# The output shift of a fused decoder layer: from VectorE's loop to rows written early and accumulating stores of GpSimd

## What is computed

```
x = x + gt1 * mix
h2 = modulate(rmsnorm(x, norm2_g), sh2, sc2)
ffn = hierarchical_moe(h2, ...)
x = x + gt2 * ffn
mod_f = silu(c) @ w_ada_final + b_ada_final
sh_f, sc_f = split(mod_f, 2)
out = modulate(rmsnorm(x, norm_f_g), sh_f, sc_f)

def modulate(hf, shift, scale):
    return hf * (1.0 + scale) + shift
```

## Time and profile before

| | before |
|---|---|
| median of three runs | 1040.6 us |
| the profiled execution's own time | 1039.79 us |
| its span, first to last instruction | 1038.0 us |
| busy: TensorE / VectorE / ScalarE / GpSimd | 981.2 / 797.5 / 530.4 / 109.1 us |
| mean granted TensorE clock | 0.992 of full speed |
| bytes moved by DMA | 206.78 MB |
| tail: first `YG` load issued | 992.6 us |
| tail: TensorE's first and last weighted sum | 998.2 and 1027.6 us |
| tail: VectorE's last instruction ends | 1034.85 us |

### The profile page before, as it was taken

How to read it: one execution, slowest core, us unless ns; L and a number is a source line. 1 busy time by engine, 2 the same in 40 slices (tenths; PEclk the granted TensorE clock), 3 DMA queues, 4 the chain that set the end, 5 groups by cost and what they waited for, 6 DMA issues and landing times.

```text
span 1038.0 us, 15568 instructions
## 1 busy us (share of the span) xinstructions
PE 981.2 (95%) x5698; PEld 771.5 (74%) x5698; DVE 797.5 (77%) x1486; ACT 530.4 (51%) x930; POOL 109.1 (11%) x151
## 2 busy tenths in 40 slices
PE   5899998999899999999999999899999999999996
PEld 5669688978897998989988888466666666666642
DVE  7859879836983886958676768898888888787828
ACT  4555532654275555555663323465665656565522
POOL 0201101000100000010010000121221221212100
PEclk9899999999999999999999999999999999999998
DMA  9823633232324233230185434589999999999375
GB/s 364 250 80 105 199 105 103 62 101 61 105 61 122 82 93 111 62 102 1 58 333 164 183 141 182 186 292 363 372 370 367 372 366 358 368 355 349 105 306 205
DMA packets 81033, 206.78 MB, mean 199 GB/s; under 512 B 11878, under 2 KB 40630, under 8 KB 72780
## 3 DMA queue, kind: packets, MB, share of 16 engines
q1 hardware_dynamic: 59232, 156.25, 41.8%
q0 software_dynamic: 15120, 43.72, 13.2%
q10 hardware_dynamic: 6620, 6.00, 1.8%
HBM read 189.61 MB, written 24.71 MB: 206 GB/s over the span
## 4 chain that ended last, share of the span: by engine, by line
PE 66%; DVE 15%; DMA 10%; ACT 4%; issue 3%; SPq 1%; ACTq 0%; DVEq 0%; POOLq 0%
PE PS L1999 13%; PE PS L2001 12%; PE PS L2000 12%; DMA WGU<-in_w_exp_up 7%; PE PS L2297 4%; PE PS L2083 3%; PE PS L2305 3%; PE PS L2303 3%; PE PS L2304 3%; DVE AT L1466 3%; PE PS L2288 2%; PE PS L2408 1%; DVE ACC L1264 1%; DMA AST<-in_w_ada 1%; PE PS L2133 1%
## 5 line engine op out<-in xcount | busy, mean ns | idle before, releaser
L1999 PE MATMUL PS<-WH,HT 128*128 128x256 f32 x512 | 146.8, 287 | 1.3 <-ACT GVH L924 1.3
L2000 PE MATMUL PS<-WL,HT 128*128 128x256 f32 x512 | 144.8, 283 | 0.0
L2001 PE MATMUL PS<-WH,HL 128*128 128x256 f32 x512 | 144.8, 283 | 0.0
L1825 DVE TENSOR_TENSOR WGL<-WGU,WGH 128x1024 fp32r<-128x1024 f32 x96 | 116.9, 1219 | 18.1 <-ACT WGH L1171 16.8
L1466 DVE COPY_PREDICATED AT<-MASK,PS 128x64 f32<-128x64 uint8 x320 | 72.8, 228 | 63.1 <-PE PS L2094 44.0
L1171 ACT ACTIVATE WGH<-WGU 128x1024 fp32r<-128x1024 f32 x96 | 98.5, 1064 | 33.6 <-DMA WGU<-in_w_exp_up 28.1
L1999 PEld LDWEIGHTS PS<-WH,HT 128*128 128x128 f32 x512 | 98.2, 192 | 4.0 <-issue 4.0
L2000 PEld LDWEIGHTS PS<-WL,HT 128*128 128x128 f32 x512 | 98.2, 192 | 0.0
L2001 PEld LDWEIGHTS PS<-WH,HL 128*128 128x128 f32 x512 | 98.1, 192 | 0.0
L2303 PE MATMUL PS<-WGH,XGTH 128*96 128x512 f32 x192 | 88.3, 460 | 0.0
L1863 DVE TENSOR_TENSOR WDL<-WDN,WDH 128x2048 fp32r<-128x2048 f32 x32 | 73.4, 2293 | 17.6 <-ACT WDH L1181 17.5
(11 more groups left out here) (355 smaller groups left out, 2259.0 us busy)
## 6 DMA issues: line engine op xcount, KB each, us to landing
WGU<-in_w_exp_gate SPq DMA_DIRECT2D x32, 1024.0 KB, 12.6
WGU<-in_w_exp_up SPq DMA_DIRECT2D x32, 1024.0 KB, 18.5
WDN<-in_w_exp_down SPq DMA_DIRECT2D x32, 1024.0 KB, 13.5
AR<-in_w_ada POOLq DMA_DIRECT2D x32, 512.0 KB, 4.2
WF<-in_w_in SPq DMA_DIRECT2D x28, 512.0 KB, 5.6
AST<-in_w_ada SPq DMA_DIRECT2D x16, 512.0 KB, 8.6
AR<-in_w_ada_final POOLq DMA_DIRECT2D x16, 512.0 KB, 4.7
YG<-expert_rows SPq DMA_DIRECT2D x8, 1024.0 KB, 12.3
```

What stands on the lines that cost most here:

```text
L1825: V.tensor_tensor(WGL[s][:, :, ks, :], WGU[s][:, :, ks, :], WGH[(NCH * s + c) % 4][:].bitcast(F32), ALU.subtract).then_inc(wgl_ready, 1)
L1999: MM(ps, wh, xh, start=first, stop=False)
L2000: MM(ps, wh, xl, start=False, stop=False)
L2001: return MM(ps, wl, xh, start=False, stop=last)
```

## The change

The final shift is no longer added by VectorE. Instead:

- GpSimd's queue, behind its last `store_gain`, waits until all six gains are stored and then issues eight DMAs, DRAM to DRAM, each writing row 2 of `gain_d` (the shift) into the 128 output rows of one tile (4 KB a row, 512 KB a DMA).
- At the end of its program, behind `extras_done`, GpSimd waits for those eight (`shift_st`), and then for each tile waits for `out_scaled` and issues the store of `OUTT[t % 4]` with `accum_op=add`: the DMA adds what it brings to what stands in the output.
- SP's eight plain stores, VectorE's `shifted`, the semaphore `out_ready`, the tile `SHF` and its load on ScalarE's queue are gone. VectorE's wait for `rows_in` is 16 in place of 32.

```diff
@@ sync
             for t in range(NT):
                 sp.dma_start(YG[t][:, :, :], ys_rows[:, 0:3:2, t, :]).then_inc(yg_in[t], 16)
-            for t in range(NT):
-                sp.wait_ge(out_ready, t + 1)
-                sp.dma_start(out_rows[:, t, :], OUTT[:, t % 4, :]).then_inc(out_st[t % 4], 16)
             for s in range(4):
                 sp.wait_ge(out_st[s], 16 * NT // 4)
@@ gpsimd
             for i, g in ((1, GT2), (2, SHC), (3, GSC)):
                 store_gain(i + 2, i, g)
+            pool.wait_ge(gain_st, 96)
+            for t in range(NT):
+                pool.dma_start(out_rows[:, t, :], gain_d[2:3, :].to_broadcast([P, D])).then_inc(shift_st, 16)
...
             pool.sem_inc(extras_done, 1)
+            pool.wait_ge(shift_st, 16 * NT)
+            for t in range(NT):
+                pool.wait_ge(out_scaled, t + 1)
+                pool.dma_start(out_rows[:, t, :], OUTT[:, t % 4, :], accum_op=ALU.add).then_inc(out_st[t % 4], 16)
@@ scalar
-            for i, dst in ((3, GSF), (2, SHF)):
-                act.dma_start(dst[:], gain_d[i:i + 1, :].to_broadcast([P, D])).then_inc(rows_in, 16)
+            act.dma_start(GSF[:], gain_d[3:4, :].to_broadcast([P, D])).then_inc(rows_in, 16)
@@ vector
-            def shifted(t):
-                v_.wait_ge(out_scaled, t + 1)
-                V.tensor_tensor(OUTT[:, t % 4, :], OUTT[:, t % 4, :], SHF[:], ALU.add).then_inc(out_ready, 1)
-
-            v_.wait_ge(rows_in, 32)
+            v_.wait_ge(rows_in, 16)
...
                                        op0=ALU.mult, op1=ALU.mult).then_inc(out_scaled, 1)
-                shifted(t)
```

More of the change, by code:

```diff
@@ L303, in layer_kernel @@
         assert BASE + small_at[0] * KB <= nc.sbuf_usable_end
-        SHF = at("SHF", 168, [P, D])
         GSF = at("GSF", 172, [P, D])
@@ L530, in layer_kernel @@
         out_scaled = sem("out_scaled")
-        out_ready = sem("out_ready")
+        shift_st = sem("shift_st")
         out_st = [sem(f"out_st{s}") for s in range(4)]
```

## The result

| | before | changed |
|---|---|---|
| median | 1040.49 us (20 runs, 1037.71 to 1043.39) | 1044.43 us (20 runs, 1041.42 to 1048.95) |
| ratio to before | | 1.004, 95% interval 1.003 to 1.005 |
| profiled execution, its span | 1039.79, 1038.0 us | 1044.46, 1042.6 us |
| first load of expert rows issued | 992.6 us | 992.6 us |
| from there to the end of the span | 45.4 us | 50.0 us |

The change makes the kernel slower by 3.9 us, 0.4%. Forecast was 0.5 us faster, within what can't be told from no change. Both profiled executions issue the first load of expert rows at the same time, so the whole of the 4.6 us between the two spans lies in the tail.

What follows compares the result with a forecast made beforehand. VectorE bounds the tail and gains 3.5 us; full DMA engines then put the last landing at 1037.0 against 1037.5, so -0.5 us: 1039.3 profiled, 1040.1 median. Own range 1038.7 to 1044.9; eight in ten 1038.2 to 1050.5.

Steps and rivals of the forecast that it cites:

- What bounds the tail, what VectorE gains: Tail: VectorE is the bound; without the shift, rounds take 3.6 us and it ends 3.5 us sooner, not 10.
- x: DMA engine time of one accumulating 512 KB store in the tail: put at 2.6 us, against 1.3 for a plain one.
- the forecast's own case: Tail stores: x from 1.8 to 3.2 us, change from -1.9 to +4.3 us; chance 0.6.
- Rival 2: Tail stores: two reads and the write do not overlap, x 3.9 us, DMA engines become the bound, +9.9 us; chance 0.2.
- rival 3: Tail stores: the add's second read is hidden, x 1.3 us, change -2.4 us; chance 0.15.
- The queue of stores: Tail: DMA engines busy with loads and stores without a gap from 1008.5 to 1036.2 us, last landing at 1037.0.
- The landing: Last accumulating store lands about 4.8 us after issue: 1.4 to start, 2.6 of data, 0.8 after the last packet.
- Loads late for TensorE: Tail: stores on another queue delay the expert-row loads, so TensorE ends late, about 2.5 us on top; chance 0.05.
- the last store alone: Last store without the queue: issued at 1031.65, data through at 1035.65 us after 1.4 and 2.6 us.
- Nothing stands behind the accumulating stores on GpSimd's queue: End of GpSimd's program: no later work there waits behind the stores, so this was costed at nothing.
- The early writes at nothing: Eight shift writes on GpSimd from about 577 us, 4 MB: costed at nothing, at most 10 us if cover were gone.

Runs made afterwards that it cites:

- e6: The kernel before with the shift left out of the output altogether, stores by SP; median 1038.13 us against 1040.67 for before, ratio 0.9972.
- e3: The changed kernel, with GpSimd also waiting for all stores to land before its program ends; median 1047.89 us against 1041.43 for before, ratio 1.0061.
- e1: The kernel before plus one 4 KB DMA issued by GpSimd behind the last scaling; median 1048.44 us against 1041.43 for before, ratio 1.0067.
- e2: The changed kernel with plain stores on GpSimd's queue in place of accumulating ones; median 1042.54 us against 1041.43 for before, ratio 1.0008.
- e5: The kernel before, with GpSimd only waiting for the last scaling before it ends, no DMA added; median 1046.16 us against 1040.67, ratio 1.0052.
- e4: The kernel before plus the eight early writes of the shift, overwritten later by its plain stores; median 1040.56 us against 1041.43, ratio 1.0007.
- e8: The changed kernel with GpSimd adding only tiles 2 to 4, VectorE shifting and SP storing the others; median 1036.66 us against 1040.67 for before, ratio 0.9959.
- e9: Repeat of e8, the same kernel measured again; median 1038.73 us against 1040.47 for before, ratio 0.9984.

## Why the prediction was wrong

- **What bounds the tail, what VectorE gains**: right. Rounds of 3.56 us where 3.6 was worked out, only 3.5 of 10 us able to come out (e6: 3.5 us from the first load's landing to VectorE's end, 3.1 us of the tail).
- **x, the engine time of an accumulating store**: 2.9 us where 2.6 was put down. It lies in the forecast's own case (1.8 to 3.2), at the point from which the prediction called the change slower. Rival 2 (3.9 us) and rival 3 (hidden) both fall. A plain store takes 1.3 us of the engines, this one 2.2 times that. The rule of the Trainium skill (Collectives: The Full Stack, section "The bandwidth ceiling: the fold count and why AG ≠ RS ≠ AR"), that an add halves the rate through its second read, agrees with this.
- **The queue of stores**: it was to end last, busy without a gap until 1036.2. With x at 2.87 the same sum gives a landing at 1008.5 + 6.9 + 23.0 + 0.8 = 1039.2. Instead the strip falls to 2 tenths at 1033.1 to 1034.0, before the last store's data, and the landing comes 0.6 us sooner than by that sum: the engines had slack, and it was the late issue of the last store that set the last landing.
- **The landing**: 5.8 us for the last store where 4.8 was put together, and 5.1 in e3. Some 0.3 of that is x; what the rest is, and why the two executions differ, stays open.
- **Loads late for TensorE** (rival 4, given 0.05): happened, but for 1.1 us and not 2.5. It was treated as a case of its own, though even at x = 2.6 the engines are full by the forecast's own sum, and what is served later must be somebody's; it should have been a term. The slowest load landed after 25.6 us in place of 18.3. The rule of the Trainium skill that the engines go round their queues (DMA: Bandwidth & Descriptors, "Queues, rings and completion order") agrees with that.
- These make the last landing 1.1 us later than before instead of 0.5 sooner: the last store alone was to land at 1036.45, and VectorE's 1.1 us and the landing's 1.0 bring it to 1038.6. With that alone the kernel would have been 1 us slower, within the range of "same".
- **"Nothing stands behind the accumulating stores on GpSimd's queue"**: this is the step that failed. The end of the program stands there, with a DRAIN of 7 to 11 us. It adds the time from Sync's readiness at 1038.7 to 1042.4, 3.7 us, more than all other errors together (1.6 us). In all five runs in which this DRAIN ends last (changed, e1, e2, e3, e5) the span ends 0.2 us behind it. The trace of before had the row (10.1 us at 989.5) but I read no closing instructions, and the description of the kernel before calls `extras_done` GpSimd's last work; I took an idle GpSimd for a free one.
- The early writes at nothing: right (e4).

Forecast: 1037.0 for the last landing plus 0.5 to the end. Measured: 1038.6, and 4.0 to the end. The measured median of 1044.43 lies inside the forecast's own range of 1038.7 to 1044.9. That is luck: the upper end stood for x = 3.2 and full DMA engines, and most of the loss is the DRAIN, which no term of the sum and no rival has.

Open: what the DRAIN does in its 7 to 11 us, and why its length differs between kernels (6.9 in e4, 10.8 in e1). It is not mere scatter. The three kernels whose GpSimd issues the same DMAs agree closely (before 10.117, e5 10.113, e6 10.113 us), though the last DMA was just issued in two of them and 45 us old in the third; e8 and e9, one kernel, have 9.03 and 8.89. But the changed kernel and e3, which also issue the same DMAs, have 9.65 and 7.58, so the DMAs alone don't set it, and more of them doesn't mean longer.

## What to carry to other kernels

An engine that finished long ago may have closing work behind it that nobody saw: before the last work of a kernel is handed to GpSimd, look up the length of its last DRAIN, and keep GpSimd's last instruction that much (here 11 us) ahead of the end. Offload as many items of a loop as the next bound asks for, and not the last ones: three tiles of eight gave 1.7 to 2.0 of the 3.1 us that there were to gain, and the last tiles stayed on the engines whose programs end at once. An accumulating store saves an engine's add, but costs the DMA engines 2.2 times a plain store here, and takes about twice as long to land.

## What the runs showed of the hardware that was not expected

- GpSimd's closing DRAIN took 6.9 to 10.8 us in the eleven profiles here, whether the last DMA was just issued (10.8, 9.6, 8.1), had just landed (7.6) or was 45 us old (10.1). In the five in which it ended last, the kernel's end waited for it. The DRAINs of the others ended with their last instruction: TensorE's, 5.4 or 7.9 us long, with its matmuls, ScalarE's (0.23 us) and VectorE's (1.3) with theirs; in e6, where VectorE's started behind its last instruction, it took 0.017 us. Sync's took 0.013.
- A plain store of 512 KB by GpSimd lands after 2.9 us and SP's after 2.6; the prediction had put 3.5 together (1.4 + 1.3 + 0.8), from a load and a scatter. An accumulating one lands after 5.1 to 6.3 us with few others under way (the last of e3, the three of e8 and of e9), and keeps the 16 engines busy for 2.9 us against 1.3.
- Accumulating stores beside loads made the last load of expert rows land after 25.6 us in place of 18.3, plain stores of the same queue after 21.0 without delaying TensorE.
